# First weight sum of the seven-product slots made by two transfers instead of by GpSimd

## The reference

```python
y, yc = token_mixers(h @ w_in[l], hc @ w_in[l], b_gate[l], ...)
x = x + g1 * (y @ w_out[l])
h = rmsnorm(x, norm2_g[l]) * (1.0 + sc2) + sh2
x = x + g2 * sq_relu_mlp(h, w_mlp1[l], w_mlp2[l])
```

```python
h = h + (gate * hr) @ w_out
h = h + swiglu(rms_norm(h, a_ffn_norm[i]), a_ffn_w_in[i], a_ffn_w_out[i])
k, v = shared_kv(h, kv_norm, w_kv, k_norm, cos, sin)
h = h + dilated_attention_mixer(...)
h = h + swiglu(rms_norm(h, b_ffn_norm[j]), ...)
```

## Time and profile before

| | |
|---|---|
| median of 3 runs | 3291.73 us (3286.6 to 3291.94) |
| profiled execution, first to last instruction | 3286.2 us; no time of its own is given for what lies around the span |
| TensorE busy | 3255.1 us |
| VectorE busy | 2027.2 us |
| GpSimd busy | 1028.5 us |
| ScalarE busy | 730.0 us |
| read from HBM | 292.84 MB, 90 GB/s |

### The profile page before, as it was taken

How to read it: one execution, slowest core, us unless ns; L and a number is a source line. 1 busy time by engine, 2 the same in 40 slices (tenths; PEclk the granted TensorE clock), 3 DMA queues, 4 the chain that set the end, 5 groups by cost and what they waited for, 6 DMA issues and landing times. The chain is left out here.

```text
span 3286.2 us, 40354 instructions
## 1 busy us (share of the span) xinstructions
PE 3255.1 (99%) x15522; PEld 2464.8 (75%) x15522; DVE 2027.2 (62%) x3686; ACT 730.0 (22%) x1567; POOL 1028.5 (31%) x806
## 2 busy tenths in 40 slices
PE   8999999999999999999999999999999999999999
PEld 6767775555555566788888854888886887888888
DVE  8766777676765624278545656756536688866543
ACT  3432422010101333131111124211101235321111
POOL 0111323323232010224444401444441453344443
PEclk9999999999999999999999999999999999999999
DMA  6434412333331121332222221222223221122222
GB/s 261 138 102 128 126 52 79 114 122 110 119 107 55 61 88 49 97 87 78 90 90 90 80 87 64 80 88 90 90 90 101 81 82 53 40 77 90 90 90 90
DMA packets 66896, 304.51 MB, mean 93 GB/s; under 512 B 8496, under 2 KB 21168, under 8 KB 40720
## 3 DMA queue, kind: packets, MB, share of 16 engines
q1 hardware_dynamic: 54368, 268.68, 24.3%
q0 software_dynamic: 6528, 18.75, 1.8%
q10 hardware_dynamic: 5808, 14.49, 1.3%
HBM read 292.84 MB, written 2.88 MB: 90 GB/s over the span
## 5 line engine op out<-in xcount | busy, mean ns | idle before, releaser
L2857 POOL TENSOR_TENSOR scratch<-ring 128x512 f32<-128x512 f32 (+1 forms) x160 | 217.1, 1357 | 1443.6 <-PE psum L744 952.9
L744 PE MATMUL psum<-big,scratch 128*128 128x256 f32 (+1 forms) x2240 | 606.9, 426 | 0.0
L744 PEld LDWEIGHTS psum<-big,scratch 128*128 128x128 f32 x2240 | 425.6, 190 | 163.7
L744 PE MATMUL psum<-H,scratch 128*128 128x256 f32 (+1 forms) x2144 | 498.9, 387 | 0.0
L744 PEld LDWEIGHTS psum<-H,scratch 128*128 128x128 f32 x2144 | 406.5, 190 | 77.0 <-issue 5.0
L744 PE MATMUL psum<-big,ring 128*128 128x256 f32 (+1 forms) x1584 | 421.4, 418 | 6.6 <-DVE cb L2172 2.5
L744 PE MATMUL psum<-H,ring 128*128 128x256 f32 (+1 forms) x1536 | 396.2, 400 | 1.7 <-issue 0.7
L744 PEld LDWEIGHTS psum<-big,ring 128*128 128x128 f32 x1584 | 300.1, 190 | 111.9 <-DVE cb L2172 3.7
L1480 ACT ACTIVATE cb<-psum 128x256 f32<-128x256 f32 x336 | 129.0, 384 | 1011.0 <-PE psum L744 1011.0
L744 PEld LDWEIGHTS psum<-H,ring 128*128 128x128 f32 x1536 | 290.0, 190 | 76.8 <-ACT H L1578 6.4
L713 PE MATMUL psum<-H,ring 128*128 128x512 f32 x736 | 328.6, 598 | 0.0
(11 more groups left out here) (397 smaller groups left out, 4144.6 us busy)
## 6 DMA issues: line engine op xcount, KB each, us to landing
ring<-in_wall SPq DMA_DIRECT2D x202, 1024.0 KB, 4.9
big<-in_wada SPq DMA_DIRECT2D x48, 512.0 KB, 3.5
big<-in_wada POOLq DMA_DIRECT2D x32, 512.0 KB, 4.1
big<-in_wada SPq DMA_DIRECT2D x8, 1024.0 KB, 21.1
scratch<-in_rpb ACTq DMA_DIRECT2D x16, 512.0 KB, 4.0
big<-big ACTq DMA_DIRECT2D x64, 64.0 KB, 4.9
X<-in_xin SPq DMA_DIRECT2D x4, 768.0 KB, 6.9
scratch<-negd SPq DMA_DIRECT2D x8, 384.0 KB, 9.1
```

The lines of the kernel that those rows point to most:

```text
L744: mm = pe.matmul(fast_bank(st, q, b), lhsT, rhs(k), start=start and k == 0, stop=k == kt - 1, skip_group_check=True)
L2857: pool.tensor_tensor(s1, a21, a22, ALU.add).then_inc(combo_own, 1)
```

## The change

The first sum, s1 = a21 + a22, isn't computed by GpSimd any more. SP copies a21 from `wall` in HBM straight into the buffer of s1 (256 KB), and GpSimd then issues an accumulating transfer that adds a22 from HBM to it (256 KB). The copy of slot n is issued right behind the ring load of slot n+1 and waits for product 7 of slot q-2, and at the starts of stages for the same gates as GpSimd (`first_term`). GpSimd waits for the copy (`first_term_in`), issues the accumulating transfer, makes s3, waits until the transfer has landed (`second_term_in`), and makes s2 and s4. So that a21 and a22 are contiguous in HBM, the host lays out each fast slot by blocks, a11, a21, a12, a22, each 128 partitions by four blocks of 128 floats (with kt = 3 the fourth is zeros); the ring load stays 1 MB. Semaphores of the opening's loads are used again.

```diff
+            def first_term(n):
+
+                q = FAST[n]
+                if q >= 2:
+                    sp.wait_ge(prod[7], q - 1)
+                for l in range(DEPTH):
+                    if n == Y[l].slot0:
+                        sp.wait_ge(pv_done, 8 * l + 8)
+                if n == YA.slot0:
+                    sp.wait_ge(lru_v, DT)
+                if n == HEADS.slot0 + 1:
+                    sp.wait_ge(q_ssq, 1)
+                if n == YB.slot0:
+                    sp.wait_ge(aO, len(ATTN))
+                sp.dma_start(combos[q % 2][:, 0, :, :], wall[n][:, 512:1024].rearrange("p (k c) -> p k c", k=4))\
+                  .then_inc(first_term_in[q % 2], 16)
...
                 sp.dma_start(ring[:, r * SLOT:(r + 1) * SLOT], wall[n]).then_inc(arrived[r], 16)
+                if n - 1 in FAST:
+                    first_term(n - 1)
...
             assert mod_at == MOD_TILES
+            first_term(N_SLOTS - 1)
...
+            def fast_block(r, b, k):
+                at = r * SLOT + (b * 4 + k) * P
+                return ring[:, at:at + P]
...
-                        lhsT = combos[q % 2][:, cols, k, :] if cols < 4 else \
-                            slot_cols(r, (cols - 4) // 2 * kt + k, (cols - 4) % 2 * P, P)
+                        lhsT = combos[q % 2][:, cols, k, :] if cols < 4 else fast_block(r, cols - 4, k)
...
-                    pool.tensor_tensor(s1, a21, a22, ALU.add).then_inc(combo_own, 1)
+                    pool.wait_ge(first_term_in[q % 2], 16 * (q // 2 + 2))
+                    pool.dma_start(combos[q % 2][:, 0, :, :], wall[slot][:, 1536:2048].rearrange("p (k c) -> p k c", k=4),
+                                   accum_op=ALU.add).then_inc(second_term_in[q % 2], 16)
                     pool.tensor_tensor(s3, a11, a21, ALU.subtract)
-                    pool.wait_ge(combo_own, mixes + 1)
+                    pool.wait_ge(second_term_in[q % 2], 16 * (11 + q // 2 + 1))
                     pool.tensor_tensor(s2, s1, a11, ALU.subtract).then_inc(combo_own, 1)
-                    pool.wait_ge(combo_own, mixes + 2)
+                    mixes += 1
+                    pool.wait_ge(combo_own, mixes)
                     pool.tensor_tensor(s4, a12, s2, ALU.subtract).then_inc(combos_ready, 1)
-                    mixes += 2
...
+    for st in STAGES:
+        for x, (kind, g, s) in enumerate(st.slots()):
+            kt = st.k_half(kind, g)
+            whole = wall[st.slot0 + x].reshape(P, 8, 2, P)
+            blocks = np.zeros((P, 4, 4, P), np.float32)
+            for b in range(4):
+                blocks[:, b, 0:kt] = whole[:, b // 2 * kt:(b // 2 + 1) * kt, b % 2]
+            wall[st.slot0 + x] = blocks.reshape(P, SLOT)
```

More of the change, by code:

```diff
@@ L287, in build @@
         consts_in = sem("consts_in")
-        x_in = [sem(f"x_in{g}") for g in range(4)]
+        x_in = [sem(f"x_then_terms_in{g}") for g in range(4)]
         bias_in = [sem(f"bias_in{b}") for b in range(4)]
@@ L293, in build @@
         first_in = [sem(f"first_in{g}") for g in range(4)]
-        mod_in = [[sem(f"mod_in{q}_{r}") for r in range((MOD_RING, 4)[q])] for q in range(2)]
+        mod_in = [[sem(f"mod_then_terms_in{q}_{r}") for r in range((MOD_RING, 4)[q])] for q in range(2)]
+        second_term_in = mod_in[0][0:2]
         mod_used = sem("mod_used")
@@ L370, in build @@
         combo_own = sem("combo_own")
+        first_term_in = x_in[0:2]
         gate_in = [sem(f"gate_in{a}") for a in range(2)]
@@ L2842, in mix_weights @@
                     r, kt = slot % RING, st.k_half(kind, g)
-                    a = ring[:, r * SLOT:(r + 1) * SLOT].rearrange("p (k f c) -> p k f c", k=8, f=2)
-                    a11, a12, a21, a22 = a[:, 0:kt, 0, :], a[:, kt:2 * kt, 0, :], a[:, 0:kt, 1, :], a[:, kt:2 * kt, 1, :]
+                    a = ring[:, r * SLOT:(r + 1) * SLOT].rearrange("p (b k c) -> p b k c", b=4, k=4)
+                    a11, a21, a12 = (a[:, b, 0:kt, :] for b in (0, 1, 2))
                     s1, s2, s3, s4 = (combos[q % 2][:, i, 0:kt, :] for i in range(4))
```

## The result

The changed kernel takes 3350.22 us in the median (3346.91 to 3354.04), the kernel before beside it 3289.16 us: ratio 1.0189, 95% interval 1.0176 to 1.0201, so 61 us slower. The forecast was +13.1 us. Sign and range hold, the size doesn't. The profiled execution has a span of 3349.3 us against 3286.2, 63.1 us more; that is the sum to be explained.

What follows compares the result with a forecast made beforehand. TensorE was taken as the bound, busy 3255.1 of 3286.2 us. Stalls of 4.2 + 6.6 + 2.3 = 13.1 us, contention 0, on 3291.73 gave 3304.8 us (+0.40%), range 3294 to 3394.

Steps and rivals of the forecast that it cites:

- The sign set for being wrong at the root: Prediction fails at its root if T isn't 3.0 to 4.5 us, or the copy lands over 6.5 us after the load.
- T: Time of the 256 KB accumulating transfer on GpSimd's queue, taken as 3.8 us.
- The chain of an ordinary slot: Ordinary narrow slot: load issue, copy, accumulating transfer, sums two and four take 12.7 us of 13.4 available; it holds.
- rival C: In the 124 narrow slots the chain passes 13.4 us and becomes the bound; 74 us at T = 5.5, 3366; chance 0.30.
- (a): First out slot of each relu-stage group, product 5 before product 2: short by 1.06 us, four times, 4.2 us.
- (b): Last four, three-block slots of each gated stage: every second one stalls, 3 x 2.2 = 6.6 us.
- (c): Start of stage YB at its gate: chain of 9.6 us against 7.36 available, short by 2.3 us.
- (d): Less contention between GpSimd's sums and VectorE: at most 7.3 us won, taken as 0.
- Traffic: HBM reads up by 160 x 0.52 MB = 84 MB; contention term taken as 0.
- A: Transfers are quick, T of 2.2 to 3.0 us: no measurable change, 2 to 6.6 us, 3297; chance 0.20.
- D: Faster: VectorE waits go and T is 2.8 us or less, 2 us won, 3290; chance 0.03.
- E: Stage HEADS: swaps behind GpSimd's sums delay VectorE's copies out of PSUM; 20 us on top, 3325; chance 0.05.

Runs made afterwards that it cites:

- copy-only: Changed kernel without the accumulating transfer: SyncE still copies a21 behind the ring load, GpSimd adds a22 onto the copy itself; 3356.0 us, 1.0221.
- late-sums run: Kernel before, no transfers: GpSimd makes all four sums from the ring, but starts only when the next slot's ring load has landed; 3325.1 us, 1.0116.
- run with traffic alone: Sums as in the kernel before, plus both transfers at 192 KB each into columns nobody reads, nobody waiting for their data; 3289.0 us, 1.0004.
- early-copy kernels: Changed kernel with the copy issued ahead of the ring load, 3319.6 us, 1.0100; also with YB's first slot by GpSimd alone, 3311.9 us, 1.0072.

## Why the prediction was right and where it failed

Where the sum had 13.1 us behind late sums, 22 came; the other 41 us have no term in it at all, 25 of them VectorE's and 11 the clock's. The sign set for being wrong at the root, T outside 3.0 to 4.5, didn't come (T was 4.0), because it looked at the transfers alone. One small misreading stands at the start: among line 744's waits the second longest total, 2.0 us, has no releaser named, and isn't VectorE's.

*The chain of an ordinary slot: right.* The copy landed 5.5 us behind the load's issue (5.7 forecast), the accumulating transfer took 4.0 (3.8), two sums and their handover 2.7 (2.9). A plain 256 KB transfer took 3.3 us where I had 2.8, and the accumulation 0.7 on top where I had 1.0. Only one handover was off: between the copy's landing and the start of the next transfer's issue lie 0.64 us in the median, not the 0.14 that I had taken from a wait for TensorE. That belongs to the issue and not to landings as such: the second sum starts 0.07 us after its transfer's landing in the changed kernel, the first 0.16 after the copy's in the copy-only one, where my expectation had put 0.6. 12.9 us against 12.7 of 13.4: narrow slots don't stall in general, and rival C didn't come. In 13 of the narrow slots the copy landed 6.4 to 7.2 us after its own issue; six ordinary ones waited 0.3 to 1.2 us for it, and a late slot 2.05; I had no term for that. Rival C's pieces of 512 bytes didn't come either: by the packet counts of the profile each transfer moved its 256 KB in 128 packets, thus 2 KB each.

*(a) and (b), late and three-block slots: right place, 1.4 times the size.* 10.8 us forecast, 15 measured by taking them out. In the trace TensorE loses 0.9, 2.2 and 1.0 us, and 2.3, 1.0 and 2.2: 9.6 in all, the pattern of every second three-block slot among them. The fourth late slot waited for VectorE instead (0.56 us). Two half-clock stretches behind them add 3.4; the rest is within what is uncertain.

*(c) the gate of YB: right place, a fifth of the size.* 2.3 us forecast, 12 measured. Four terms failed in a row: the copy landed after 4.07 us (2.7), with the load and the copy of the next slots issued 0.37 and 0.84 us behind it; the transfer's issue began 0.9 us after that (0.14); the transfer took 4.6 (3.8); and the second sum ran 4.03 us instead of 1.35. Beside it stood eight VectorE instructions with two inputs in SBUF and no gap between them:

```profile
2883.14 4.03 POOL L2887 TENSOR_TENSOR scratch<-scratch,ring 128x512 f32<-128x512 f32 x1 [2.41 <-DMA scratch<-in_wall]
2883.29 2.76 DVE L2084 TENSOR_TENSOR X<-H 128x256 f32<-128x256 f32 x8
```

In the kernel before, GpSimd's sums there were over before this line's first instruction began. Here VectorE keeps its pace (2.76 us for eight) and the sum ends 1.1 us after the last of them. I had put the sums in "at their undisturbed length".

*(d) contention 0: the step that failed, and the largest.* I asked only what sums taken away from GpSimd would save VectorE (at most 7.3 us), and not where the remaining ones would come to lie. The row was there: an add of VectorE took 1.37 us beside a GpSimd sum. In the changed kernel the third sum of the narrow slot above runs from 2241.42 to 2242.99, beside product 7 of the slot before it (2241.44 to 2243.33): the place where in the output stages VectorE's chain ahead of line 2197 runs. The price by itself is 37 us in the late-sums run; in the changed kernel the waits on VectorE grew by some 25 us. By the ratios of the runs, the cost of 62 us goes in these steps: 29 when the copy comes early (waits on GpSimd, their clock, and part of the displacement), 9 more with YB's slot, 18 more when the sums are back in their place, and 6 stay.

*The clock: no term at all.* The half-clock stretches add about 11 us. Three stalls of 2.05 to 2.4 us are followed by 3.4 us at half speed, which loses another 1.7 each.

*Traffic: right.* HBM reads grew by 83.9 MB (84 forecast), and by the run with traffic alone three quarters of them cost nothing.

*Rivals.* A and D fell with T = 4.0. C fell; the plain transfer did show a steep price of the chain (24 us for 0.8 us, thus 30 for each us, where C had 55), but at T below C's bound, and without stalls in every second slot. E had the right stage and not the size: 9 us where it had 20. By the trace 5.0 us of waits on VectorE's line 2184 (0.9 before) and 2.2 on GpSimd stand there; whether the swaps are behind them wasn't run apart. That 3350 lies inside the range is owed to C's chance, thus to a cause that didn't act.

*Open.* How VectorE's 25 us divide between the moved sums of the output stages, those beside the wide stage's modulation tiles and those of the head slots wasn't run separately. Nor was why the copy lands late in 13 slots. The early-copy kernels also have many stalls of 0.2 us behind line 2194 and smaller ones, some 8 us in all, whose cause is open. A step between two runs is a difference of ratios that are each known to 0.1 or 0.15%, so some 5 us of each step are uncertain.

## What to carry to other kernels

Moving work of an engine costs by its new neighbours: before a helper engine's work is shifted, lay its new window over the instructions for which the bounding engine waits, and ask which of them share a port with it. If a helper's work must be fed by a transfer, start the transfer so early that the work stays in its old window (here, from the last reader of the buffer and not from the last reader of the set). And where the work taken off an engine isn't on the path, the best to be had is no change: the best version with the transfers took 3293 us against 3288.

## What the runs showed of the hardware

- An accumulating transfer of 256 KB holds GpSimd for 0.89 us of issue and lands 4.0 us after it begins, a plain one 0.56 and 3.3; beside a 1 MB load the accumulating one takes 6.4.
- GpSimd starts a sum 0.07 to 0.16 us after a transfer's landing and 0.14 after TensorE's signal, but the issue of a transfer only 0.6 us after the landing that it waits for.
- Beside a GpSimd sum VectorE's 128x256 additions of two SBUF inputs take 1.37 us instead of 0.42, those with a PSUM input 0.42 as ever; the stretched ones end about 0.3 us after the sum. GpSimd's own sum took 4.03 us instead of 1.27 where VectorE had eight such instructions without a gap.
- The granted clock fell to 0.50 for 6.8 us from inside a wait of TensorE of 7.5 us, and for 3.4 us behind three of 2.05 to 2.4 us; behind two as long it didn't.
